# Two expert layers of a transformer kernel: six experts in two rounds of three, with 64, 32 and 32 columns, instead of three rounds of two

## What is computed

```python
def grouped_moe_2(h, router_w, router_b, w_gate, w_up, w_down):
    aff = jax.nn.sigmoid((xf @ router_w).astype(jnp.float32))
    biased = (aff + router_b).reshape(T, N_GROUPS, EXPERTS_PER_GROUP_2)
    grp_score = jnp.sum(lax.top_k(biased, TOP_K)[0], axis=-1)
    g_sel = jnp.argmax(grp_score, axis=-1)
    local = lax.top_k(biased[tok, g_sel], TOP_K)[1]
    expert = g_sel[:, None] * EXPERTS_PER_GROUP_2 + local
    w = aff[tok[:, None], expert]
    w = w / jnp.sum(w, axis=-1, keepdims=True)
    ...
    def expert_block(args):
        xb, e = args
        hid = jax.nn.silu(xb @ w_gate[e]) * (xb @ w_up[e])
        return hid @ w_down[e]
    ...
    out = jnp.zeros((T, D)).at[tok_buf].add(ys * w_buf[:, None])
```

## Time and profile before

| | us |
|---|---|
| median of three executions | 1863.09 |
| lowest, highest | 1862.43, 2954.26 |
| the profiled execution's own time | 1866.2 |
| its span, first to last instruction | 1864.4 |
| TensorE busy (matmuls) | 1694.4 (91%) |
| VectorE busy | 761.8 (41%) |
| ScalarE busy | 398.7 (21%) |
| GpSimd busy | 92.8 (5%) |
| mean rate of the DMA engines | 310 GB/s |

### The profile page before, as it was taken

The page is one execution under the profiler, slowest core; times in us unless marked ns, Lnnn a source line. Parts: engine busy times, 40 slices in busy tenths (PEclk is TensorE's granted clock), DMA queues, the critical chain, the costliest instruction groups (busy, mean ns, idle before and its releaser), DMA issues.

```text
span 1864.4 us, 20556 instructions
## 1 busy us (share of the span) xinstructions
PE 1694.4 (91%) x8053; PEld 982.3 (53%) x8053; DVE 761.8 (41%) x1621; ACT 398.7 (21%) x761; POOL 92.8 (5%) x144
## 2 busy tenths in 40 slices
PE   8999989999799998899886999799998788799995
PEld 5587754343456776444335876444443564454342
DVE  1678742221356766222116356532221644512223
ACT  1232321111022232111103355011110341111111
POOL 1111100000110110000001000000000100000000
PEclk9999979999899999899997999799999899799998
DMA  9868599999974875799996521497999741679995
GB/s 380 343 236 323 226 330 410 421 421 421 420 295 149 321 272 215 316 422 421 421 423 255 194 78 67 182 360 284 423 421 423 277 181 67 263 291 383 421 422 240
DMA packets 83739, 578.84 MB, mean 310 GB/s; under 512 B 8896, under 2 KB 13232, under 8 KB 28336
## 3 DMA queue, kind: packets, MB, share of 16 engines
q1 hardware_dynamic: 60624, 500.20, 66.2%
q0 software_dynamic: 16416, 63.97, 9.1%
q10 hardware_dynamic: 6592, 13.20, 2.1%
HBM read 574.13 MB, written 3.20 MB: 310 GB/s over the span
## 4 chain that ended last, share of the span: by engine, by line
PE 73%; DMA 15%; DVE 7%; ACT 2%; issue 2%; SPq 0%; POOL 0%; POOLq 0%; DVEq 0%; ACTq 0%
PE bank L767 70%; DMA ring<-in_weights 12%; DMA hi_ring<-in_weights 2%; PE bank L799 2%; DVE mix L1943 1%; DVE work L1801 1%; ACT work L1388 1%; DMA consts<-in_cst 1%; ACT mix L1388 1%; DVE mix L1801 1%; DVE small L1801 1%; PE bank L895 0%; DVE oT L1979 0%; DVE x L1801 0%; DVE small L1952 0%
## 5 line engine op out<-in xcount | busy, mean ns | idle before, releaser
L767 PE MATMUL bank<-ring,work 128*64 128x512 f32 (+2 forms) x1516 | 390.5, 584 | 23.7 <-DMA ring<-in_weights 22.3
L1388 ACT ACTIVATE work<-bank 128x512 f32<-128x512 f32 (+6 forms) x234 | 123.4, 531 | 831.6 <-PE bank L767 427.1
L767 PEld LDWEIGHTS bank<-ring,work 128*64 128x64 f32 (+2 forms) x1516 | 141.4, 144 | 252.7 <-issue 243.4
L767 PE MATMUL bank<-ring,oT 128*64 128x512 f32 (+1 forms) x864 | 221.2, 596 | 11.0 <-DMA ring<-in_weights 9.0
L1801 DVE TENSOR_TENSOR work_parts<-bank,work_parts 128x512 fp32r<-128x512 f32 x68 | 47.0, 692 | 370.6 <-ACT work_parts L1388 370.6
L767 PE MATMUL bank<-work_parts 128*128 128x256 f32 (+2 forms) x612 | 151.5, 357 | 21.6 <-DVE work_parts L2029 18.9
L767 PE MATMUL bank<-hi_ring,work 128*64 128x512 f32 (+1 forms) x608 | 154.3, 596 | 7.5 <-DMA hi_ring<-in_weights 6.0
L767 PEld LDWEIGHTS bank<-ring,oT 128*64 128x64 f32 (+1 forms) x864 | 76.1, 144 | 137.4 <-issue 136.8
L767 PEld LDWEIGHTS bank<-work_parts 128*128 128x128 f32 x612 | 108.2, 205 | 70.5 <-issue 37.8
L2118 DVE SCALAR_TENSOR_TENSOR work<-bank,small,work 128x512 f32<-128x512 f32 x34 | 25.5, 751 | 282.7 <-PE bank L767 213.6
L767 PE MATMUL bank<-ring,xT 128*128 128x512 f32 (+2 forms) x352 | 139.0, 554 | 1.7 <-DVE xT L2261 1.7
(11 more groups left out here) (236 smaller groups left out, 2052.2 us busy)
## 6 DMA issues: line engine op xcount, KB each, us to landing
ring<-in_weights SPq DMA_DIRECT2D x244, 1024.0 KB, 15.2
hi_ring<-in_weights SPq DMA_DIRECT2D x118, 1024.0 KB, 16.0
ring<-in_weights SPq DMA_DIRECT2D x52, 2048.0 KB, 10.5
hi_ring<-in_ada POOLq DMA_DIRECT2D x38, 512.0 KB, 11.8
mod_rows<-in_ada POOLq DMA_DIRECT2D x25, 512.0 KB, 6.1
work<-in_ada POOLq DMA_DIRECT2D x22, 512.0 KB, 6.1
hi_ring<-in_weights SPq DMA_DIRECT2D x5, 2048.0 KB, 10.6
work<-in_vecs POOLq DMA_DIRECT2D x8, 1024.0 KB, 7.5
```

Of the source, the lines that this page charges most:

```text
L767: ins = nc.tensor.matmul(o, lhsT, rhs, start=start, stop=stop)
L1388: return nc.scalar.activation(o, i, f, **kw)
```

## The change

In layers e and o the rounds are now: the pair of experts 0 and 1; a triple (positions 10, 11, 12 of the order); the largest lone expert; a triple (13, 14, 15); the second lone expert; then three pairs. Eight rounds in place of nine, still five sets and 48 pieces. In a triple the first expert has room for 64 tokens (columns 0 to 63), the other two for 32 each (64 to 95 and 96 to 127). A table `rank_of` sends the experts of rank 11 and 13, 14 to the first triple and 12, 15, 16 to the second, so that the four smallest experts get the 32-column places. A triple's pieces are whole matrices, three per kind; a kind waits for all three before its first matmul, and releases them together.

```diff
@@ -91,7 +91,7 @@
-    return [pair[0], (2,), (3,), *pair[2:]] if tag in SORTED else pair
+    return [pair[0], (10, 11, 12), (2,), (13, 14, 15), (3,), *pair[2:5]] if tag in SORTED else pair
...
+COLUMNS = {1: [(0, P)], 2: [(0, CAP), (CAP, CAP)], 3: [(0, CAP), (CAP, CAP // 2), (CAP + CAP // 2, CAP // 2)]}
+
+
+def whole(tag, r):
+
+
+    return len(ROUNDS[tag][r]) != 2
...
+    put("rank_of", np.tile([*range(1, 12), 13, 14, 12, 15, 16], (P, 1)))
...
-                    if len(kinds[r]) == 1:
-                        w = take(what, r, h).rearrange("p (c n) -> p c n", c=chunks)
-                        return [(range(chunks), slice(0, P), w)]
+                    if whole(tag[0], r):
+                        return [(range(chunks), slice(at, at + n), take(what, r, e).rearrange("p (c n) -> p c n", c=chunks))
+                                for e, (at, n) in enumerate(COLUMNS[len(kinds[r])])]
...
-                        release[0] += 2
+                        release[0] += 2 * len(of) if whole(tag[0], r) else 2
...
-                    two = len(kinds[r + 1]) == 2
+                    two = not whole(tag[0], r + 1)
...
-                        cs("iota")[:, 0:NEXP].unsqueeze(2).broadcast_to([P, NEXP, NEXP]), ALU.is_equal))
+                        cs("rank_of").unsqueeze(2).broadcast_to([P, NEXP, NEXP]), ALU.is_equal))
...
+                    step(tt(room, room, sm("key"), ALU.subtract))
+                    step(v.tensor_scalar(sm("key"), sm("pos"), 12.5, float(CAP // 2), ALU.is_gt, ALU.mult))
...
-                    rows = P if len(kinds[sets[j][0]]) == 1 else CAP
...
+                                same = [a for a, (_, rows) in enumerate(of) if rows == of[-1][1]]
+                                for kin in ([a for a in range(len(of)) if a not in same], same):
...
-                for a, p in enumerate(ROUNDS[tag][r]):
-                    one = len(ROUNDS[tag][r]) == 1
+                one = whole(tag, r)
+                for a, p in enumerate(ROUNDS[tag][r][h:h + 1] if one else ROUNDS[tag][r]):
```

More of the change, by code:

```diff
@@ L145, in ring_plan @@
             j = min(usable, key=lambda k: held[k])
-            pair = m >= first and len(ROUNDS[tag][MOE_PIECES[tag][m - first][1]]) == 2
-            landed[j] += 32 if pair else 16
+            both = m >= first and not whole(tag, MOE_PIECES[tag][m - first][1])
+            landed[j] += 32 if both else 16
             slot.append(j)
@@ L181 @@
     ("lncount", 2 * NT * 33), ("before", P), ("iota", P), ("ones", 2), ("half", 16), ("tie", NEXP), ("third", NEXP),
-    ("stack", NEXP), ("earlier", 16)])
+    ("stack", NEXP), ("earlier", 16), ("rank_of", NEXP)])
 PARAM, PARAM_N = layout([
@@ L961, in places @@
                                                 for s_ in range(n) for T in range(NT)])
-                    product(f"{tag}.sg{j}", [(2 * s_, 2 * s_ + 2, P,
+                    product(f"{tag}.sg{j}", [(4 * s_, 4 * s_ + max(2, len(kinds[r])), P,
                                               [(pick[:, T, s_ * P:(s_ + 1) * P],
-                                                (gate_at(tag) if j else gate_of)[:, T, kinds[r][0]:kinds[r][0] + 2]) for T in range(NT)])
-                                             for s_, r in enumerate(sets[j])])
+                                                (gate_at(tag) if j else gate_of)[:, T, kinds[r][0]:kinds[r][0] + max(2, len(kinds[r]))])
+                                               for T in range(NT)]) for s_, r in enumerate(sets[j])])
                 def take(what, r, h):
@@ L987, in gate_up @@
                     name = f"{tag}.{what}{r}"
-                    for h in range(len(kinds[r])) if parts is None else parts:
+                    for h in ((0,) if whole(tag[0], r) else (0, 1)) if parts is None else parts:
                         o = begin(name) if h == 0 else psum[banks.jobs[name][0]]
@@ L1546, in places @@
                                             lambda t: t[:, 0:n * NT * P].rearrange("p (s n) -> p s n", s=n))])
[L1547 to L1551, removed]
+                    carry(f"{tag}.sg{j}", [(slot_gate[at:at + rows, home + s_:home + s_ + 1], lambda t, s_=s_, a=a, at=at, rows=rows:
+                                            t[at:at + rows, 4 * s_ + a:4 * s_ + a + 1])
+                                           for s_, r in enumerate(sets[j]) for a, (at, rows) in enumerate(COLUMNS[len(kinds[r])])])
                 def sig(r):
@@ L2096, in picks @@
                 def picks(j):
-                    first, n = kinds[sets[j][0]][0], sum(len(kinds[r]) for r in sets[j])
-                    rows = P if len(kinds[sets[j][0]]) == 1 else CAP
+                    alike = len({len(kinds[r]) for r in sets[j]}) == 1
                     for dest in (pick_parts, pick):
                         for T in range(NT):
[L2102 to L2105, removed]
+                            for s_, r in enumerate(sets[j][0:1] if alike else sets[j]):
+                                n, of = len(sets[j]) if alike else 1, COLUMNS[len(kinds[r])]
+                                first = kinds[r][0]
+                                to = dest[:, T, s_ * P:(s_ + n) * P].rearrange("p (s n) -> p s n", s=n)
+                                slots = (slot_at(tag) if j else slot)[:, T, first:first + n * len(of)].rearrange("p (s a) -> p s a", s=n)
+                                same = [a for a, (_, rows) in enumerate(of) if rows == of[-1][1]]
+                                for kin in ([a for a in range(len(of)) if a not in same], same):
+                                    if not kin:
+                                        continue
+                                    at, rows = of[kin[0]]
+                                    ins = tt(to[:, :, at:at + rows * len(kin)].rearrange("p s (a n) -> p s a n", a=len(kin)),
+                                             cs("iota")[:, 0:rows].unsqueeze(1).unsqueeze(1).broadcast_to([P, n, len(kin), rows]),
+                                             slots[:, :, kin[0]:kin[-1] + 1].unsqueeze(3).broadcast_to([P, n, len(kin), rows]),
+                                             ALU.is_equal)
+                            ins.then_inc(pick_ready, 1)
                 def gathered(j):
```

## The result

| | us |
|---|---|
| before, median | 1864.12 (4 runs) |
| changed kernel, median | 1912.24 (1910.20 to 1912.92, 4 runs) |
| ratio, with its 95% interval | 1.0257 (1.0245 to 1.0269) |
| predicted | 1910, range 1850 to 1945 |
| profiled execution of the changed kernel | 1911.97, span 1910.1 |

One of the four executions of before took 2954.26 us, which its median hardly shows.

The account below looks back on a forecast made before the run. The stage was taken as bound by TensorE first and DMA last. Per layer, 95.4 us added less 62.1, 2.8 and 7 gives +23.5, so +47 for two layers on 1863: 1910 us, range 1850 to 1945.

Parts of the forecast that it names:

- A triple's kind: One gate, up or down of a triple on TensorE: widths take turns, 1.99 us a chunk, 15.9 us for eight.
- the ends of the bound: A triple's gate, up or down on TensorE: 6.9 us if all three experts share steps, 15.9 if widths never share.
- the 1067.51 row: Trace row of 64-column records before 15-column ones, read as the array emptying before a width change; load starts 0.06 us after.
- The sum: Expert stage per layer: 95.4 us added, 62.1 removed, 2.8 and 7 saved; +23.5 us, +47 for two layers.
- late waits go, -7: End of each expert stage: most of TensorE's 8.4 us of waiting for DMA goes, -7 us per layer.
- Lost transfer time: DMA in layer e's stage: transfer time lost rises from 19 to some 40 us.
- What was taken at nothing: VectorE masks, SyncE table reads, freeing of pieces, evacuations: counted as zero, together bounded at -1 to +4 us per layer.
- A: Triple's matmuls: different widths in different columns share a step, 6.9 us per gate, up or down; 1834 us, chance 0.15.
- C: Triple's matmuls: a matmul's two records are taken apart, four width changes a chunk; 1936 us, chance 0.10.
- D: Triple's matmuls: widths take turns but changing between 64 and 32 is free, 13.8 us; 1885 us, chance 0.10.
- B: Triple's matmuls: the three share but stagger, three steps a chunk, 10.3 us; 1856 us, chance 0.05.
- some 4 to 5 us of the lost time stay: DMA under A: of 19.0 us lost in layer e's stage, some 4 to 5 remain (first slots, three at once).

Follow-up runs that it names:

- x1: Changed kernel with all matmuls of a triple's 64-column expert first, then those of its two 32-column experts: 1890.37 us, ratio to before 1.0137.
- x4: Kernel before, with only the second expert of round 6 in layers e and o split into two 32-column matmuls: 1898.56 us, ratio 1.0182.
- x2: Changed kernel with a triple's 64-column expert computed as two 32-column matmuls, so four tiles of one width: 1842.30 us, ratio to before 0.9884.
- x5: The kernel of x2 run again, unchanged, as the measure for x6 and x7: 1843.34 us, ratio to before 0.9889.
- x7: The kernel of x2 with one pair moved ahead of the first triple: 1831.67 us, ratio to before 0.9826.
- x3: Kernel before, with each 64-column matmul of rounds 6 to 8 in layers e and o split into two of 32: 1864.58 us, ratio 1.0000.
- x6: The kernel of x2 with each lone expert's round ahead of its triple: 1842.76 us, ratio to before 0.9880.

## Why the prediction was right

It forecast 1910 us and slower; 1912.24 was measured. Step by step:

- **A triple's kind, 15.9 us.** Right, in the mechanism and in the number: 1.98 us a chunk measured, 1.99 forecast. Its two parts were tested apart: x1 gives 0.13 us a change, and the 2 + 2 steps stand in the timeline. The choice between the ends of the bound (6.9 or 15.9) carried the whole forecast. It was read from changes between 128 and 64 and between 64 and 15 columns; the question those rows left open, whether disjoint columns help, is answered by the trace after and by x1 and x4: they don't. So taking this side at 0.60 was a judgment that the rows before could not settle. One of its supports was misread: the 1067.51 row is of weight loads, and 1067.82 is where they end. The four 64-column matmuls themselves start at 1067.51 and take 0.42 us by their own row, so until 1067.93 by a modelled end, and the 15-column load at 1067.88 does not stand clear of them. The 0.15 us for 128 and 64 columns don't need that row. The Trainium skill, "TensorEngine Tiling (Array Packing)", Tiling Modes, says that changing the tiling mode drains the engine. The traces agree for 64 and 32 columns too: the load of each width waits for the other width's steps, and a change costs 0.13 us.
- **The sum.** +23.5 us a layer forecast; the stages grew by 22.7 and 22.9. The part "late waits go, -7" was short by about 1 (8.4 us of them stood in the earlier trace rows, and TensorE is now busy for all 50 us from 1400 to 1450), which is most of the difference.
- **Lost transfer time.** "Some 40 us" forecast, 38 measured.
- **What was taken at nothing.** VectorE's masks, in the timeline of after:

```profile
1215.47 1.04 DVE L1809 TENSOR_TENSOR work_parts<-consts,small 128x64 fp32r<-128x64 f32 x6 [2.03 <-PE bank L777]
1216.42 1.03 DVE L1809 TENSOR_TENSOR mod_rows<-consts,small 128x64 f32<-128x64 f32 x6
```

  They take 2.07 us in place of 1.51, end at 1217.45, and the gather starts at 1222.3: covered. The first load of the first triple went out at 1212.79, before at 1213.26. Counted from the first group of round 0 that is 5.2 us for 4.7, but SyncE's queue had waited 2.0 us for a slot by then, 0.6 before: the three reads of the table fit into that wait.
- **The rivals.** A (free sharing) needed three weight loads within some 20 ns; the 64-column one and the 32-column ones start 1.0 us apart. C (four changes a chunk) would be 18 us a kind; there are two changes. D (turns, but free changes) would be 13.8; x1, which has nearly no changes, is close to D's condition, and measured 1890 where D was worked out as 1885. Under D it would have equalled the changed kernel. B (staggered) is excluded by the same rows.
- **What was sized wrong.** The price of rival A, 1834 us: the kernel that realises its condition (x2) takes 1842. The term that was too small is "some 4 to 5 us of the lost time stay": in layer e it was 7.6 us in x2 and 8.6 in x5, the same kernel. The order of x7 removes nearly all of it. In the prediction's first paragraph "nine tenths of nearly every slice" is too much: the earlier trace rows has a 9 in 25 of 40 slices and 7 or 8 in the others; nothing hangs on it.

## What to carry to other kernels

Before packing narrow operands side by side into the array, look at whether they have one width. Here, four tiles of 32 columns cost the same as two of 64 (x3), and the same two steps of 0.43 us as a single 128-column matmul, but one of 64 beside two of 32 costs 2.3 times as much; splitting the wide one turned a loss of 2.6% into a gain of 1.2%. And when the compute falls below the transfers, look at the transfer time lost early in the stage, while the first buffers come free: moving one pair ahead gave another 0.6%.

## What the runs showed of the hardware that was not expected

- In no row read here did tiles of different width in disjoint columns run together, and even their weight loads waited: pauses of 0.81 to 0.84 us between loads, for 0.29 among tiles of one width. I had given free sharing 15%.
- Splitting a 64-column matmul into two of 32 is free in time (x3: 1.0000, 0.9991 to 1.0010), though it doubles matmuls and weight loads.
- A long wait for a piece is followed by slow matmuls: in x2, after 6.99 us without matmuls, the granted clock was 0.50 from 1272 to 1274, with steps of 0.82 us, close to what half the clock (1.2 GHz for 2.4) makes of 0.43. In the kernel before the clock is 1.00 in all three windows of the earlier trace rows; there no wait for a load from 1230 to 1450 is longer than 1.3 us.
- Not settled: why x6's order lost no more transfer time than x5's (13.3 and 13.1 us from 1210 to 1310), while the ring model put it 5 us later in total.
